# Feed-forward gate and up products with one 512-column matmul per weight block for both halves of the input

## What is computed

```python
def swiglu(xn, w_gate, w_up, w_down):
    return (jax.nn.silu(xn @ w_gate) * (xn @ w_up)) @ w_down

h = h + swiglu(rmsnorm(h, ffn_norm[l]), w_gate[l], w_up[l], w_down[l])
```

## Time and profile before

| | us |
|---|---|
| median of three runs | 1037.84 |
| the three runs | 1038.17, 1036.15, 1037.84 |
| the profiled execution's own time | 1035.64 |
| its span from first to last instruction | 1033.9 |
| granted TensorE clock, mean over the span | 0.996 |

### The profile page before, as it was taken

The page is one execution under the profiler, slowest core; times in us unless marked ns, Lnnn a source line. Parts: engine busy times, 40 slices in busy tenths (PEclk is TensorE's granted clock), DMA queues, the critical chain, the costliest instruction groups (busy, mean ns, idle before and its releaser), DMA issues.

```text
span 1033.9 us, 21970 instructions
## 1 busy us (share of the span) xinstructions
PE 1016.0 (98%) x8296; PEld 989.5 (96%) x8296; DVE 661.0 (64%) x1219; ACT 556.8 (54%) x947; POOL 54.7 (5%) x76
## 2 busy tenths in 40 slices
PE   7999999999999999999999999999999999999997
PEld 7999899999999999999999999999999899999996
DVE  5545987775555558666476565648877676565654
ACT  6566786564444446565564444448566564444443
POOL 2021000120000002000010000002100020000000
PEclk9999999999999999999999999999999999999999
DMA  9634344466555555334455555555653445646531
GB/s 342 224 126 143 122 144 159 147 205 197 168 194 172 193 171 181 108 123 145 142 173 183 180 184 180 183 182 166 208 170 109 137 142 185 202 163 200 166 122 41
DMA packets 49208, 172.76 MB, mean 167 GB/s; under 512 B 5376, under 2 KB 7680, under 8 KB 49024
## 3 DMA queue, kind: packets, MB, share of 16 engines
q1 hardware_dynamic: 48096, 170.93, 49.5%
q10 hardware_dynamic: 1056, 1.05, 0.5%
HBM read 169.86 MB, written 1.05 MB: 165 GB/s over the span
## 4 chain that ended last, share of the span: by engine, by line
PE 93%; DVE 4%; ACT 2%; DMA 0%; issue 0%; POOLq 0%; SPq 0%; POOL 0%; ACTq 0%; DVEq 0%
PE bank L307 91%; DVE w_lo L1141 1%; PE bank L497 1%; DVE a_lo L1153 1%; DVE arena_r L1153 1%; DMA xT<-xT_dram 0%; ACT w_hi L787 0%; DVE xT L1170 0%; DVE arena L1134 0%; DVE tmp L1134 0%; ACT L973 0%; DVE arena L1400 0%; ACT soft_p L877 0%; ACT a_hi L827 0%; DVE arena L1388 0%
## 5 line engine op out<-in xcount | busy, mean ns | idle before, releaser
L787 ACT ACTIVATE w_hi<-stage 128x1024 fp32r<-128x1024 f32 x319 | 334.3, 1053 | 189.4 <-PE bank L307 186.0
L307 PE MATMUL bank<-a_hi,w_hi 128*128 128x256 f32 x1488 | 425.6, 287 | 8.2 <-ACT a_hi L987 7.4
L307 PE MATMUL bank<-a_hi,w_lo 128*128 128x256 f32 x1488 | 420.1, 283 | 0.0
L307 PE MATMUL bank<-a_lo,w_hi 128*128 128x256 f32 x1488 | 415.0, 283 | 0.0
L1141 DVE TENSOR_TENSOR w_lo<-stage,w_hi 128x1024 fp32r<-128x1024 f32 x319 | 387.2, 1230 | 10.5 <-ACT w_hi L787 10.3
L307 PE MATMUL bank<-arena_r,w_hi 128*128 128x256 f32 x1840 | 337.1, 285 | 0.8 <-DVE arena_r L1153 0.7
L307 PEld LDWEIGHTS bank<-a_hi,w_hi 128*128 128x128 f32 x1488 | 286.4, 192 | 12.3 <-DVE w_lo L1141 7.9
L307 PEld LDWEIGHTS bank<-arena_r,w_hi 128*128 128x128 f32 x1840 | 286.9, 192 | 2.5 <-DVE arena_r L1153 0.9
L307 PEld LDWEIGHTS bank<-a_hi,w_lo 128*128 128x128 f32 x1488 | 286.4, 192 | 0.0
L307 PEld LDWEIGHTS bank<-a_lo,w_hi 128*128 128x128 f32 x1488 | 283.3, 192 | 1.3 <-issue 1.2
L307 PE MATMUL bank<-arena_r,w_lo 128*128 128x256 f32 x920 | 259.3, 283 | 0.0
(11 more groups left out here) (151 smaller groups left out, 720.5 us busy)
## 6 DMA issues: line engine op xcount, KB each, us to landing
stage<-slab_dram SPq DMA_DIRECT2D x319, 512.0 KB, 3.5
con<-con_dram SPq DMA_DIRECT2D x1, 1153.5 KB, 10.9
xT<-xT_dram SPq DMA_DIRECT2D x4, 256.0 KB, 5.3
arena<-arena ACTq DMA_DIRECT2D x2, 512.0 KB, 7.9
out_dram<-arena SPq DMA_DIRECT2D x8, 128.0 KB, 2.0
vec<-vec_dram SPq DMA_DIRECT2D x1, 245.5 KB, 3.7
pos<-pos_dram SPq DMA_DIRECT2D x1, 128.0 KB, 10.7
```

Source lines behind the costliest of these rows:

```text
L307: return nc.tensor.matmul(out, lhsT, rhs, start=start, stop=True, skip_group_check=True)
L787: nc.scalar.activation(w_hi[:, slot, :], stage[:, slot, :], ACT.Copy).then_inc(hi_made, 1)
```

## The change

The input of the feed-forward part, `a_hi` and `a_lo`, becomes one tile, `a_pair`, with 512 columns for each chunk (256 of hi, then 256 of lo). A gate or up slab runs `wide_slab`: for each block one matmul of 512 columns with `w_hi` (hi by hi to the first half of the bank, hi by lo to the second) and one of 256 columns with `w_lo` (added to the first half). Two matmuls and two weight loads stand where there were three of each. The halves are added afterwards: ScalarE copies the second half to `low` (`low_out`), VectorE adds it to the first (`both_halves`), and the scaling by `rB`, or the product with the silu, is now an operation of its own on the sum.

The first two slabs of each feed-forward part stay as they were, and so does the very last up slab of each. The down slab of p = 1 is run one slab later: the order is now gate 0, up 0, down 1 of the round before, gate 1, up 1, down 0. The loads follow the new order; the slabs in memory keep theirs.

```diff
-        a_hi = sb("a_hi", [P, NC, TOK], f32r)
-        a_lo = sb("a_lo", [P, NC, TOK], f32r)
+        a_pair = sb("a_pair", [P, NC, 2 * TOK], f32r)
+        a_hi, a_lo = a_pair[:, :, 0:TOK], a_pair[:, :, TOK:2 * TOK]
...
+        low = chunks(arena, 9216, 4)
...
+            def ffn_loads(base):
+
+                for n in range(base, base + 5):
+                    load(n, n)
+                with sp.Fori(0, NG - 1) as i:
+                    for c, shift in enumerate((1, 1, -2, 0, 0, 0)):
...
+            def wide_slab(n, slot, out):
+
+                pe.wait_ge(lo_made, n + 1)
+                for k in range(NC):
+                    w = slice(k * P, k * P + P)
+                    mm(out[:, :], w_hi[:, slot, w], a_pair[:, k, :], k == 0)
+                    last = mm(out[:, 0:TOK], w_lo[:, slot, w], a_hi[:, k, :], False)
+                last.then_inc(slab_done, 1)
...
+            def ffn_round(f, base, i, last=False):
+
+                n, q = base - 1 + 6 * i, 22 * f + 2 * i
+                slot = [(base - 1 + c) % SLOTS for c in range(6)]
                 for p in range(2):
...
+                    pe.wait_ge(gu_taken, q + p - 1)
+                    wide_slab(n + 3 * p, slot[3 * p], bank[4 + 2 * p])
+                    pe.wait_ge(ff_made, q + p - 1)
+                    if last and p:
+                        column_slab(n + 4, slot[4], half(7, 0))
+                    else:
+                        wide_slab(n + 3 * p + 1, slot[3 * p + 1], bank[5 + 2 * p])
+                    if p == 0:
+                        pe.wait_ge(fflo_ready, q)
+                        row_slab(n + 2, slot[2], *ff(1), False)
                 if last:
...
+                    last_rows(n + 5, [ff(0), ff(1)],
+                              *([(done, q + 1), (done, q + 2)] for done in (ffhi_ready, fflo_ready)))
                     return
...
+                pe.wait_ge(fflo_ready, q + 1)
+                row_slab(n + 5, slot[5], *ff(0), False)
 
             def ffn(f, base):
-                ffn_round(f, base, 0, first=True)
+                q = 22 * f
+                if f:
+                    pe.wait_ge(ff_made, q)
+                first_column_slabs(base, [half(4, 0), half(5, 0)], 2 * f + 1)
+                norm_sum(2 * f + 1)
+                wide_slab(base + 2, (base + 2) % SLOTS, bank[6])
+                pe.wait_ge(r_ready, 2 * f + 2)
+                wide_slab(base + 3, (base + 3) % SLOTS, bank[7])
+                pe.wait_ge(fflo_ready, q + 1)
+                row_slab(base + 4, (base + 4) % SLOTS, *ff(0), True)
...
+            def low_out(n, i):
+
+                act.wait_ge(slab_done, n + 1)
+                nc.scalar.activation(low[:, i, :], half(4 + (0, 2, 1, 3)[i], 1), ACT.Copy).then_inc(low_taken, 1)
...
+            def ffn_round(f, base, i, last=False):
+                for c in range(5 if last else 6):
+                    n, slot, q, p = base - 1 + 6 * i + c, (base - 1 + c) % SLOTS, 22 * f + 2 * i + c // 3, c // 3
+                    if c in (1, 4):
+                        silu(q, p, gu_scaled, q - f)
+                    if c == 2 or c == 5:
+                        ff_high(q, p)
+                    if c in (0, 3):
+                        low_out(n, p)
+                    if c == 1 or c == 4 and not last:
+                        low_out(n, 2 + p)
+                    if last and c == 4:
+                        ff_high(q, p)
+                    if not last or n + SLOTS < NSLAB:
                         act.wait_ge(slab_done, n + 1)
...
+            def both_halves(out, b, i, count):
+                dve.wait_ge(low_taken, count)
+                return nc.vector.tensor_tensor(out, half(b, 0), low[:, i, :], ALU.add)
+
+            def gate(q, p, lows):
+                both_halves(tmp[:, p, :], 4 + 2 * p, p, lows + 1).then_inc(gu_taken, 1)
+                dve.wait_ge(gu_taken, q + 1)
+                times(tmp[:, p, :], tmp[:, p, :], rB[:, :]).then_inc(gu_scaled, 1)
...
+            def up(q, p, lows, ups):
+                both_halves(tmp[:, 4 + p, :], 5 + 2 * p, 2 + p, lows + 2).then_inc(up_taken, 1)
+                dve.wait_ge(up_taken, ups + 1)
+                dve.wait_ge(silu_scaled, q + 1)
+                times(tmp[:, 4 + p, :], tmp[:, 4 + p, :], tmp[:, p, :]).then_inc(ff_made, 1)
...
+                for p in range(2):
+                    q, lows = 22 * f + 2 * i + p, 41 * f + 4 * i + 2 * p - 2
+                    gate(q, p, lows)
+                    round_lo(3 * p)
+                    silu_out(q, p)
+                    if last and p:
+                        plain_up(base + 63, q, 1)
+                        ff_low(q, p)
+                        round_lo(4)
+                        return
+                    round_lo(3 * p + 1)
+                    up(q, p, lows, q - 2 * f - 1)
+                    round_lo(3 * p + 2)
+                    ff_low(q, p)
```

More of the change, by code:

```diff
@@ L584, in attend @@
                     turned(2 * soft_at[n - 2] + 1)
-            def ffn_round(f, base, i, first=False, last=False):
-                for p in range(2):
[L590 to L598, removed]
-                    column_slab(n, (base + 2 * p) % SLOTS, half(4 + 2 * p, 0))
-                    if first and p:
-                        pe.wait_ge(r_ready, 2 * f + 2)
-                    column_slab(n + 1, (base + 2 * p + 1) % SLOTS, half(5 + 2 * p, 0))
-                xs = [(ff_hi[:, p, :], ff_lo[:, p, :]) for p in range(2)]
-                n, q = base + 6 * i + 4, 22 * f + 2 * i
+            def wide_slab(n, slot, out):
[5 more added lines that the diff above has]
+                last.then_inc(slab_done, 1)
@@ L940, in rows_out, with silu, ff_high, ffn_first @@
                 attend(base + NC + 1)
-            def ffn_round(f, base, i, first=False, last=False):
-                for c in range(6):
-                    slot, n, q = (base + c) % SLOTS, base + 6 * i + c, 22 * f + 2 * i + c // 2
-                    if first and c == 1:
+            def silu(q, p, scaled, count):
+                act.wait_ge(scaled, count)
+                nc.scalar.activation(tmp[:, 2 + p, :], tmp[:, p, :], ACT.Silu).then_inc(silu_ready, 1)
+            def ff_high(q, p):
+                act.wait_ge(ff_made, q + 1)
+                nc.scalar.activation(ff_hi[:, p, :], tmp[:, 4 + p, :], ACT.Copy).then_inc(ffhi_ready, 1)
+            def low_out(n, i):
+                act.wait_ge(slab_done, n + 1)
+                nc.scalar.activation(low[:, i, :], half(4 + (0, 2, 1, 3)[i], 1), ACT.Copy).then_inc(low_taken, 1)
+            def ffn_first(f, base):
+                q = 22 * f
+                for c in range(5):
+                    n = base + c
+                    if c == 1:
                         norm_end(2 * f + 1)
@@ new lines, in ff_low, with ffn_first @@
+            def ff_low(q, p):
+                dve.wait_ge(ffhi_ready, q + 1)
+                minus_hi(ff_lo[:, p, :], tmp[:, 4 + p, :], ff_hi[:, p, :]).then_inc(fflo_ready, 1)
+            def ffn_first(f, base):
+                split_lo(base + 4, (base + 4) % SLOTS)
+                split_lo(base + 5, (base + 5) % SLOTS)
+                dve.wait_ge(r_ready, 2 * f + 2)
+                q, lows = 22 * f, 41 * f
+                plain_gate(base, q)
+                silu_out(q, 0)
+                plain_up(base + 1, q, 0)
+                ff_low(q, 0)
+                next_lo(base + 2)
+                gate(q + 1, 1, lows)
+                next_lo(base + 3)
+                silu_out(q + 1, 1)
+                up(q + 1, 1, lows, 20 * f)
+                next_lo(base + 4)
+                ff_low(q + 1, 1)
@@ new lines, in ffn_round, with round_lo @@
+            def ffn_round(f, base, i, last=False):
+                def round_lo(c):
+                    n = base - 1 + 6 * i + c
+                    if not last or n + SLOTS - LAG < NSLAB:
+                        split_lo(n + SLOTS - LAG, (base - 1 + c - LAG) % SLOTS)
+                for p in range(2):
[12 more added lines that the diff above has]
+                    ff_low(q, p)
```

109 lines of the change are left out of this document (49 added, 60 removed).

## The result

The changed kernel takes 1029.42 us (median of four, 1027.54 to 1030.30) against 1036.99 for the kernel before (four, 1035.79 to 1038.17). The ratio is 0.9928, with an interval from 0.9915 to 0.9940: 7.6 us faster. Forecast were 1023.6 and a range up to 1029.0. The sign was right; of the 13.4 us of the sum little more than half came.

A forecast was written before the change was run, and what follows sets the result against it. The loop was taken as bound by TensorE's matmul stream alone. Savings of 12.48 (wide slabs), 0.81 (down-slab waits) and 0.1 (first start) gave 13.4 us, from 1037.0 to 1023.6 us; range 1021.5 to 1029.0.

The forecast's parts named there:

- each kind keeps its own distance: Wide slabs on TensorE: a 512-column matmul takes 226.7 ns and a 256-column one 120.0, so 346.7 a pair, before 360.0.
- 12.48: Saving in us from joining matmuls: 117 wide slabs, 39 a part without the two of the start, at 0.1067 each.
- the 0.81 and 0.1 of the other terms: Savings in us: 0.81 from the second down slab's waits going, about 0.1 at the start of the first part.
- The prediction's own sign of being wrong: Loop timeline: a distance above 0.23 us behind 512-column matmuls, a late weight load, or matmuls with VectorE named ahead.
- Rival 1: 512-column matmuls run at 232 ns beside the loop's other work; 8.4 us saved, 1028.6 us; chance 0.12.
- 2: Mixed pairs stay at 360 ns, the change from long to short giving the saving back; 1036.1 us; chance 0.04.
- 3: Load of `w_lo` runs behind the 512-column matmul, not beside it; 459 ns a pair, about 1129 us; chance 0.03.
- 4: VectorE and ScalarE queues obstruct each other in the loop, TensorE waits, gain eaten; 1036 us or slower; chance 0.03.
- The start of each part: Two wide slabs save nothing in parts two and three, waiting for `ff_lo`; first part keeps about 0.1 of 0.213 us.
- Down slab one slab later: First round of each part: the second down slab's wait for `ff_lo` goes, 0.81 us in all; nothing in the loop.
- VectorE, ScalarE, banks, loads, the last round: Extra adds and copies stay hidden, VectorE busy 11.5 and ScalarE 9.3 of 16.85 us; no cost or wait elsewhere.

The follow-up runs named there:

- e2: Changed kernel with each 512-column matmul replaced by two of 256 with the same weights, slab order, copies and adds kept: 1034.52 us, ratio 0.9983 to the kernel before.
- e9: TensorE alone, computing nothing of the reference: pairs of 512 and 256 columns with varied read places; 346.7 ns a pair, but 348.3 and 350.0 with two other spacings.
- e4: Separate kernel, TensorE alone on fixed tiles, streams of several matmul lengths: 512, 256 pairs took 353.3 ns; 256 alone 120.0, 512 alone 226.7.
- e3: Changed kernel with 512 columns for the low weights' matmuls too, so every matmul of a wide slab has 512: 1126.97 us, some 227 ns a matmul.
- e12: The kernel of e9 run again, several times: five executions 207.15 to 208.60 us; the kernel's own pattern now 353.3 ns a pair, some others still 346.7.
- e5: The changed kernel itself once more, beside two other matmul orders on one chip: 1028.34 us, ratio 0.9923 to the kernel before.
- e13: TensorE alone: plain 512, 256 pairs alternating with parts of other chunk, weight or start distances; identical plain parts took 346.6 to 353.5 ns a pair.
- e16: Kernel before, with a_hi and a_lo as halves of chunks 544 columns apart in one tile, no wide slab: 1030.06 us, ratio 0.9942.
- e8: More streams on TensorE alone, computing nothing of the reference, with other length mixes: 512, 256 pairs with fixed places 346.7 ns; 512, 128 pairs 340 ns.

## Why the prediction was wrong, point by point

- **The 6.7 ns.** The step that failed is the one that takes 226.7 + 120.0 for a mixed pair, "each kind keeps its own distance". The pair takes 353.3. 117 slabs by 2.880 - 2.823 are 6.6 us, where 12.48 stood; with the 0.81 and 0.1 of the other terms that makes 7.5, against 7.6 measured. That a matmul has a price beyond its columns and that joining saves some of it was right (e2 against the changed kernel); the term was mis-sized by nearly half. The step itself does not hold even for pairs of 346.7 ns (e9): the sum comes out, but the distances are 231 and 113, 232 and 118, not 227 and 120. The prediction's own sign of being wrong, more than 0.23 behind a 512-column matmul, is what the timeline shows.
- **The row that said so.** The earlier trace rows had both numbers, 232 ns and 226.7. I took the second as the true one "because it holds steadily", and the first as a disturbance. The stream of e4 has such a course with nothing else busy: behind the turn to 512 the distances are 233, 236, 228, 233, 231, 226 and only then 226.7. And the slow nine of the earlier trace rows stand right behind the turn to 512 in their stretch (240, 235, 234, 235, 225, 230, 236, 229, 232, 231), the steady nine further on: they were the settling. In the slab a 512-column matmul is always the first behind a turn. The sample to take was the one with the slab's neighbourhood, not the steadier one.
- **Rival 1** (the slower distance, 1028.6) has nearly the right time and the wrong cause: it blamed the loop's other work, which e3 and e4 clear. Its gain of 8.4 us is 0.8 more than was measured, and the end of the range, set just behind it, fell 0.4 us short.
- **Rivals 2 to 4.** 2 has a true core, the turn of length gives something back, but half and not all. A load behind the 512-column matmul (3) and a queue in VectorE or ScalarE (4) do not show; a pair is 353 and not 459 ns, and the loop has no hole. The Trainium skill's 2.5 ns a matmul ("TensorE: Matmul & The Clock Gate", section "Back-to-back issue gap") fits none of the streams of e4: 13.3 beyond the columns at 256, 384 and 512.
- **The start of each part.** Right: the two wide slabs there save nothing, since the down slab waits for `ff_lo`. It starts 6.09 us after them, not 5.92. Of the 0.17, 0.07 is the up product, 0.53 behind the silu product instead of 0.46 (527.57 to 528.10), and 0.10 is TensorE starting its first wide slab earlier behind the norm sum, no loss.
- **Down slab one slab later.** Right: the waits are gone, and e2, with all the rest but the joining, gains 0.1 to 0.3%.
- **VectorE, ScalarE, banks, loads, the last round.** Right: 11.38 and 9.12 us busy in 17.06, `ff_lo` 5.95 us after the gate slab (forecast 5.99), and TensorE never waits in the loop.

## What to carry to other kernels

What two lengths of matmul cost when they alternate does not follow from what each costs in a row of its own; take the row with the same neighbours. Timing the pattern by itself on TensorE helps only so far: the streams of e4 forecast the slab to 0.01 us, but by those of e9, with the same pattern in the quick rhythm, it would have been 2.773 us, the prediction's error once more. So take a range from several such streams, and read the length of a slab in the kernel. Where TensorE's stream is the bound, try the order within a slab and the distance of the input chunks: 32 columns of padding brought 7 us here (6 in the kernel before), nearly as much as the change itself, though up to 1.5 us of it may be the clock.

## What was not expected of the hardware

TensorE's stream of fp32r matmuls with a weight load each has rhythms that last. The same instructions on the same places took 346.7 or 353.3 ns a pair, from one execution to another (e9 and e12, on two chips, so that the chip may have a part in it; that of e9 showed 353.3 as well, in e5) and, within one, depending on what had run ahead (e12, e13). Input chunks 544 columns apart instead of 512 make even the stream of 256 columns quicker, 119.0 ns instead of 120.0 (e16 against e2), while 576 change nothing in the kernel. Also: a 128-column matmul behind a 512-column one was followed after 60 ns (e8), while 32-column ones follow one another at 112.

What the rhythm is, inside the engine, stays open. Every stream has a weight load ahead of each matmul, so nothing here tells whether the 13.3 ns and the rhythms belong to the matmuls or to the loads. What picks the rhythm stays open too, and so does why 544 leaves the slow one and 576 does not. In the whole kernel the padding also moves every tile behind `a_pair`, among them the input of the down slabs; that was not separated from the distance. Other distances, or padding between the weight blocks, were not tried there. Nor was it shown that the changed kernel always runs in the slow rhythm: both of its profiled executions did, and the other runs are within 4 us.
